# Gate one-hots as three operations of 1024 elements with an operand in PSUM, and gate products alternating with single table rows

## The reference

```python
q = (t @ w_q).reshape(b * n, PEER_HEADS, 2, PEER_KEY_DIM)
s = jnp.einsum('thcd,hcnd->thcn', q, sub_keys)
sv, si = lax.top_k(s, PEER_TOPK)
cand = (sv[:, :, 0, :, None] + sv[:, :, 1, None, :])...
score, pos = lax.top_k(cand, PEER_TOPK)
expert = i1 * PEER_KEYS + i2          # 128 x 128 experts, 8 heads x 16 picks a token
gate = jax.nn.softmax(score, axis=-1)
...
act = gelu(einsum('td,thkd->thk', tb, take(u_tab, eb)))
return einsum('thk,thkd->td', gb * act, take(v_tab, eb))
```

## Time and profile before

| | |
|---|---|
| median of three runs | 4166.71 us |
| profiled execution | 4166.24 us |
| its span | 4164.4 us |
| TensorE busy, all of the span | 3772.8 us (91%), 22284 instructions |
| VectorE busy | 2453.1 us (59%), 4656 instructions |
| ScalarE busy | 1469.7 us (35%) |
| GpSimd busy | 727.9 us (17%) |
| mean granted clock of TensorE | 0.937 |
| lots of layer 0 | from about 1563 to 2027 us |
| lots of layer 1 | from about 3397 to 3601 us |

### The profile page before, as it was taken

The page is one execution under the profiler, slowest core; times in us unless marked ns, Lnnn a source line. Parts: engine busy times, 40 slices in busy tenths (PEclk is TensorE's granted clock), DMA queues, the critical chain, the costliest instruction groups (busy, mean ns, idle before and its releaser), DMA issues. The chain is left out here.

```text
span 4164.4 us, 58347 instructions
## 1 busy us (share of the span) xinstructions
PE 3772.8 (91%) x22284; PEld 3297.9 (79%) x22284; DVE 2453.1 (59%) x4656; ACT 1469.7 (35%) x1705; POOL 727.9 (17%) x414
## 2 busy tenths in 40 slices
PE   6986789895979999999989999999897988899999
PEld 5986579663757888888778888887766988899999
DVE  5855477737642998777315555554655798404665
ACT  4434143122423234444322222222323445443443
POOL 0100000100001553333330000000000673481000
PEclk9988699887989999999999999998998998899999
DMA  7952056410022434666655567662302546767775
GB/s 291 334 204 93 34 200 244 158 71 21 1 86 78 149 139 147 184 185 173 188 187 218 215 218 255 238 245 93 111 11 102 178 174 177 202 228 254 273 285 209
DMA packets 387378, 713.70 MB, mean 171 GB/s; under 512 B 214529, under 2 KB 267009, under 8 KB 335873
## 3 DMA queue, kind: packets, MB, share of 16 engines
q1 hardware_dynamic: 360896, 616.62, 43.7%
q0 software_dynamic: 21888, 79.70, 5.1%
q10 hardware_dynamic: 4416, 15.05, 0.9%
HBM read 605.40 MB, written 105.91 MB: 171 GB/s over the span
## 5 line engine op out<-in xcount | busy, mean ns | idle before, releaser
L2402 PE MATMUL ps<-arena_split 128*128 128x512 f32 (+1 forms) x6144 | 1069.8, 337 | 21.5 <-DVE arena_split L2375 21.5
L2402 PEld LDWEIGHTS ps<-arena_split 128*128 128x128 f32 x6144 | 948.7, 191 | 142.7 <-issue 20.1
L2192 PE MATMUL ps<-xT_split,arena_split 128*128 128x512 f32 (+1 forms) x4096 | 1025.0, 340 | 30.8 <-ACT arena L2139 17.6
L2172 POOL TENSOR_TENSOR arena_split<-ring,arena_split 128x1024 fp32r<-128x1024 f32 x256 | 645.9, 2528 | 1622.0 <-ACT arena_split L2130 1622.0
L2192 PEld LDWEIGHTS ps<-xT_split,arena_split 128*128 128x128 f32 x4096 | 715.3, 193 | 111.8 <-issue 30.5
L2192 PE MATMUL ps<-hT_split,arena_split 128*128 128x512 f32 (+1 forms) x2048 | 694.1, 339 | 0.0
L2372 DVE TENSOR_TENSOR arena_split<-ring,arena_split 128x2048 fp32r<-128x2048 f32 x128 | 293.3, 2292 | 438.2 <-ACT arena_split L2352 438.2
L273 DVE TENSOR_TENSOR arena_split<-ring,arena_split 128x2048 fp32r<-128x2048 f32 x128 | 292.4, 2291 | 351.9 <-ACT arena_split L267 351.9
L2352 ACT ACTIVATE arena_split<-ring 128x2048 fp32r<-128x2048 f32 x128 | 245.2, 1916 | 712.1 <-PE ps L2402 707.2
L2192 PEld LDWEIGHTS ps<-hT_split,arena_split 128*128 128x128 f32 x2048 | 394.6, 193 | 39.0
L267 ACT ACTIVATE arena_split<-ring 128x2048 fp32r<-128x2048 f32 x128 | 243.7, 1912 | 402.4 <-PE ps L750 155.6
(11 more groups left out here) (253 smaller groups left out, 4659.1 us busy)
## 6 DMA issues: line engine op xcount, KB each, us to landing
ring<-in_weights SPq DMA_DIRECT2D x396, 1024.0 KB, 4.9
arena<-in_side_weights POOLq DMA_DIRECT2D x152, 512.0 KB, 5.6
gates<-arena SPq DMA_DIRECT2D x48, 1024.0 KB, 6.9
activations<-arena SPq DMA_DIRECT2D x128, 256.0 KB, 2.1
arena<-gates SPq DMA_DIRECT2D x64, 512.0 KB, 5.8
arena<-activations SPq DMA_DIRECT2D x64, 512.0 KB, 7.4
activations<-arena SPq DMA_DIRECT2D x128, 128.0 KB, 2.1
arena<-gates SPq DMA_DIRECT2D x64, 256.0 KB, 5.0
```

The source lines that it names most:

```text
L2172: pool.tensor_tensor(low, self.raw(f)[:, j, :], high.bitcast(F32), ALU.subtract)\
L2192: mm = pe.matmul(k.ps[:, j, 0:self.T], self.u[:, 2 * (f % 2) + j, a, t * P:(t + 1) * P], self.h[b][:, t, :], start=n == 0, stop=n == 3 * D ...
L2402: mm = pe.matmul(k.ps[:, t, 0:self.T], self.v[:, f % 2, a, j * D + t * P:j * D + (t + 1) * P], self.weighted[:, f % 2, b, j, :], start=fir ...
```

## The change

Three things in PeerHidden:

1. The one-hots of a lot are three operations on 1024 elements (8 tokens x 128 places) in place of 16 on 128: place against row index, place against column index, and the first times the gate. The row of places (`iota`) is copied into PSUM bank 7, and the turned gates stay in PSUM bank 6, where `turn` now puts them. Each of the three has one operand in PSUM and one in SBUF.
2. The third waits for the first by a semaphore of its own (`gate_row_hots`).
3. `both` calls body and lots for one half at a time, so that TensorE, ScalarE and SP go half, lot, half, lot. VectorE and GpSimd have only the one of the two.

```diff
-        self.turned = [k.room(9216 + 512 * i, T) for i in range(3)]
+        self.turned = [k.room(9216 + 512 * i, T) for i in range(2)]
...
+        self.row_hots = k.count_of("gate_row_hots", lots)
...
         def both(*pair):
-            if body:
-                body(*pair)
-            lots(*pair)
+            for j in range(2):
+                body(*pair, halves=(j,))
+                lots(*pair, halves=(j,))
...
-            walk(eng, ROUTE_PAIRS, self.lots_to, 8, both if lots else body)
+            walk(eng, ROUTE_PAIRS, self.lots_to, 8, both if lots and body else lots or body)
...
     def sync(self, sp, load):
-        def body(c, f, i, step):
-            self.next_load(sp, c, f, load)
-            for j in range(2):
+        def body(c, f, i, step, halves=(0, 1)):
+            if halves[0] == 0:
+                self.next_load(sp, c, f, load)
+            for j in halves:
...
-        def lots(c, f, i, step):
+        def lots(c, f, i, step, halves=(0, 1)):
+            if halves[-1] == 0:
+                return
...
     def tensor(self, pe):
-            for b, route in enumerate(self.routes):
+            for bank, route in zip((2, 3, 6), self.routes):
                 for j in range(self.n):
-                    mm = pe.transpose(k.ps[:, 2 + b, j * P:(j + 1) * P], route[:, j, :], k.ident)
+                    mm = pe.transpose(k.ps[:, bank, j * P:(j + 1) * P], route[:, j, :], k.ident)
...
     def vector(self, dve):
-        for b, out in enumerate(self.turned):
-            ins = dve.tensor_copy(out, k.ps[:, 2 + b, 0:self.T])
-        chain(ins)
-        rows, columns, gates = self.turned
-        iota = k.row("iota128")
+        for b, out in enumerate(self.turned[:2]):
+            dve.tensor_copy(out, k.ps[:, 2 + b, 0:self.T])
+        iota, gates = k.ps[:, 7, 0:P], k.ps[:, 6, 0:self.T]
+        chain(dve.tensor_copy(iota, k.row("iota128")))
+        rows, columns = self.turned[:2]
...
-                for u in range(LOT):
-                    at = bass.ds(c * (2 * LOT) + ((q - 2 * ROUTE_PAIRS) * LOT + u), 1)
-                    dve.tensor_scalar(self.hot[:, q, 0, u, :], iota, columns[:, at], None, ALU.is_equal)
-                    ins = dve.tensor_scalar(self.hot[:, q, 1, u, :], iota, rows[:, at], gates[:, at],
-                                            ALU.is_equal, ALU.mult)
-                ins.then_inc(self.onehots.sem, 1)
+                at = bass.ds(c * (2 * LOT) + (q - 2 * ROUTE_PAIRS) * LOT, LOT)
+                spread = lambda x: x[:, at].unsqueeze(2).to_broadcast([P, LOT, P])
+                places = iota.unsqueeze(1).to_broadcast([P, LOT, P])
+                dve.tensor_tensor(self.hot[:, q, 1], places, spread(rows), ALU.is_equal).then_inc(self.row_hots.sem, 1)
+                dve.tensor_tensor(self.hot[:, q, 0], places, spread(columns), ALU.is_equal)
+                dve.wait_ge(self.row_hots.sem, c * 2 + self.row_hots.at(q + 1 - 2 * ROUTE_PAIRS))
+                dve.tensor_tensor(self.hot[:, q, 1], self.hot[:, q, 1], spread(gates), ALU.mult)\
+                   .then_inc(self.onehots.sem, 1)
```

More of the change, by code:

```diff
@@ L2144, in body, with lots @@
                 act.activation(self.routes[2], self.routes[2], ACT.Exp).then_inc(self.exps.sem, 1)
-        def lots(c, f, i, step):
+        def lots(c, f, i, step, halves=(0, 1)):
             u = (f - ROUTE_PAIRS) % 8
-            for q in range(2):
+            for q in halves:
                 act.wait_ge(self.products.sem, c * 2 + self.products.at(q + 1 - 2 * ROUTE_PAIRS))
```

## The result

The changed kernel takes 4111.43 us (median of 4 runs, 4107.14 to 4114.06) where the kernel before, measured with it, takes 4165.43: a ratio of 0.9865, 95% interval 0.9851 to 0.9879, so by the ratio 1.35% or 56 us faster (the two medians lie 54.0 us apart). Measured once more later (label again_after) the ratio was 0.9883, 0.9867 to 0.9900. The profiled execution took 4107.14 us, its span is 4105.3.

A forecast was written before the change was run, and what follows sets the result against it. TensorE bounds layer 0 and VectorE's one-hots held layer 1, where TensorE would take over: 32 lots × 1.80 + 31 halves × 2.88 = 146.9, plus 2 us at the start, 51 us earlier. 4166.2 − 51 = 4115 us, range 4110 to 4132.

The forecast's parts named there:

- What bounds it: PeerHidden's lots: TensorE bounds layer 0; VectorE's one-hots hold layer 1, 13.6 of every 25.14 us, until TensorE takes over.
- The one-hots' price: VectorE, each lot: three operations of 1.20 us, 3.6 us a lot against 3.64 of work before; bounds 1.20 and 2.29.
- The shut-out at 0: VectorE's one-hots no longer held up by GpSimd's subtraction: 1.55 us a lot becomes 0; bounds 0 and 2.38.
- The order: TensorE alternating half pair and lot: 0 to +3 us in layer 0, taken as 0; 4.68 us a lot in layer 1.
- the start of layer 1: Layer 1's first lot: TensorE waits 1.3 us for VectorE, then runs at half clock for a moment; 2 us added.
- The range: Whole kernel's time: 4110 to 4132 us, taking in the forecast, transfers as bound and the low part of a remaining shut-out.
- rival 1: Layer 1's lots: DMA becomes the bound, +3 to +15 us, 4118 to 4130, say 4125; chance 0.12.
- rival 2: Layer 1's lots: GpSimd's shut-out stays, VectorE is the bound at 5.15 to 5.98 us a lot, 4143; chance 0.06.
- Rivals 2 to 4: Besides rival 2: 3, PSUM operand costs two passes an element, 4184, chance 0.04; 4, VectorE's time goes by elements, 4548, 0.01.

The follow-up runs named there:

- e3: The changed kernel with its three one-hot operations and new order, but places and gates read from SBUF: 4145.83 us, ratio 0.9965 to the kernel before.
- e2: The changed kernel's new order with the old 16 one-hot operations a lot, rows, columns and gates in SBUF: 4151.52 us, ratio 0.9976 to the kernel before.
- e9: The kernel before with only GpSimd's subtraction cut to 128 of 1024 elements from the fifth pair on: 4095.9 us, ratio 0.9840 to the kernel before.
- e1: The changed kernel's three new one-hot operations in the old order, both halves and then both lots: 4106.85 us, ratio 0.9873 to the kernel before.
- e8: The changed kernel with each activation of layer 1 stored four times, three of them to a spare tensor: 4143.14 us, ratio 0.9952 to the kernel before.
- e5: The changed kernel with the last three gate pieces issued singly behind the stores of the next three pairs: 4088.88 us, ratio 0.9822 to the kernel before.
- e6: The changed kernel with the routing's comparison product and its row of 16 places moved into PSUM: 4097.93 us, ratio 0.9844 to the kernel before.

## Why the prediction was right or wrong

- **What bounds it: right.** Layer 0 gave nothing (463.0 against 463.4 us), layer 1 gave 53.9. The turn from VectorE to TensorE as layer 1's bound is the chain's.
- **The one-hots' price: right.** 1.20 us an operation against 1.21 to 1.22, 3.6 us a lot against 3.4. That fewer operations by themselves give next to nothing was a little too strict: some 6 us by e3 against e2.
- **The shut-out at 0: right**, and shown from three sides: it goes with one operand in PSUM (changed kernel), it stays with three operations in SBUF (e3), and the old operations lose it when GpSimd's are short (e9). "The two shut each other out" was too much for the lots: there VectorE's operation goes from 0.27 to over 2 us, GpSimd's stays at 2.4. The Trainium skill (SBUF — State Buffer, Who interferes with whom) says the same of one SBUF input, and the rows now bear it out for a PSUM input with an SBUF one: 288 of 288 unstretched. The Trainium skill's rule of two elements a cycle for the old form and one for the new (VectorE: DVE Perf Modes, the perf-mode tier table) did not decide, as the rows had said: e9 and the change end at the same 151 us.
- **The order: right where it counts.** No cost in layer 0, 4.66 us a lot against 4.68 in layer 1. I did not say that the alternation itself is worth nothing beside the new one-hots; e1 shows it.
- **The term that was mis-sized: the start of layer 1.** I added 2 us for a moment at half clock behind a wait of 1.3 us. TensorE waited 1.1 us, and the first lot then took 2.05 in place of 1.79, 0.3 us more (its row stands under e1 above). The measured stretch is 5.0 us up to the first lot and 146.2 behind it, 151.2, against my 5.05 + 146.9 + 2 = 153.95 (3549.7 − 3395.75). So 1.7 of the 3 us between the forecast gain of 51 and the measured 54 are the half clock, and 0.7 the lots, which took 1.79 and 2.87 us and not 1.80 and 2.88; the rest is rounding and the landmark at the end.
- **The step that failed: the range.** I wrote "The range takes in forecast and rival 1 and the low part of rival 2: 4110 to 4132", and made the sum against one profiled execution as if all outside the stage stood still. It didn't: layer 1's last transpose, ahead of all that changed there, came 5.0 us earlier in the changed kernel's profile, and 11.6 us apart in two profiles of the kernel before. Of the 7.9 us between the forecast of 4115 and the profiled 4107.1 some 3 are the mis-sized terms above and 5.0 are this. So the measured time lies at or under the lower end: the ratio gives 0.9865 × 4165.4 = 4109.2, its interval reaches down to 0.9851 × 4165.4 = 4103.4, and the profiled run took 4107.1; that the median of 4111.4 is 1.4 us inside is luck. A lower end of 4103, the forecast less the 3 us of doubt in the sum and some 9 for that scatter, would have been the honest one; all of its width had gone to the side of smaller gains.
- **Rival 1 (transfers) did not happen**, but was nearer than I made it: the share is 0.98, not near 0.9. Most of that is my rounding and my stretch: 8.7 of 9.36 us was 0.93 already, and the 94 us hold some 3% more bytes a pair than the stretch of the earlier trace rows (259 × 9.33 against 186 × 12.6). For each byte the share grew by only about 2% (0.98/259 against 0.69/186), so packets hardly slowed each other. By e8 little room is left.
- **Rivals 2 to 4 did not happen.** e3 is rival 2 in the flesh: 185.6 us against the 182 worked out for it, and 4146 us against 4143.

## What to carry to other kernels

Where an operation is now and then long by about the length of another engine's, look at that engine before making the operation cheaper: here three operations in place of 16 gave 6 us, and an operand in PSUM 34. A VectorE tensor_tensor on fp32 that runs beside GpSimd's should have one input in SBUF and the other in PSUM, if it may not wait; it costs nothing at these sizes (1208 to 1228 ns against 1218), and pays only where VectorE or what waits for it is the bound. Don't carry it over to other operations: the casts of the routing, with a single SBUF input, were shut out all the same. When one engine's gap closes, look next at what is issued in a row: four stores ahead of everything cost 18 us that no engine's busy time showed.

## What was unexpected

- A DMA share of 0.98 with TensorE undisturbed for 94 us, and of 1.01 with 2.25 us lost (e8). Of e8's 29 us only 3.9 came in the lots, 25 in the pairs behind them, where a pair is shortest.
- The gains of removed stalls are larger than the stalls: 9.0 us for 6.9 in layer 0's tail (e5), 11.0 for 8.7 ahead of layer 1's transposes (e6). In the kernel before, TensorE's transposes behind the wait last 421 ns, in e6, where the long wait is gone, 272, so part of it is the clock behind a pause; how much was not measured apart.
- In layer 1's tail it was the other way: 8.8 us came back for a stall of 10.5, since 3.0 remain.
